# A two-layer decoder step on one core: the set-up block folded into the first layer, first cache pages loaded during the last prompt head, values applied by head groups, and each value page handed back by its own products

## What is computed

```python
def pool_layer(x, buf, ...):             # layer A: D_MODEL 1024, D_A 2048
    u, z = split(rmsnorm(x) @ w_in)      # 1024 x 4096
    mix = multiscale_pool(concat(buf, u))          # trailing windows 2/4/8/16
    mix = (mix by 4 groups @ w_map) * scale
    return x + (mix * silu(z)) @ w_out, last 15 rows of concat(buf, u)
k, v = split(rmsnorm(x) @ w_kv)          # shared K/V, rows are outputs too
def diff_layer(x, k, v):                 # layer B, 8 heads of 2 x 64 (k) and 128 (v)
    q, z = split(rmsnorm(x) @ w_in_b)
    p1, p2 = softmax(q1 k1 - alibi), softmax(q2 k2 - alibi)
    o = (p1 - lam * p2) @ v
    return x + (rmsnorm(o) * silu(z)) @ w_out_b
y = rmsnorm(x) * gain                    # samples attend to cache_k/v[page_table]
```

## Time and profile before

| | us |
|---|---|
| three timed runs | 3292.47, 3285.68, 3284.3 |
| their median | 3285.68 |
| the profiled execution, its own time | 3285.73 |
| its span, first to last instruction | 3283.9 |
| PE busy | 3091.5 (94%) |
| DVE, ACT, POOL busy | 1668.1, 1278.5, 96.6 |
| mean granted TensorE clock, share of full speed | 0.971 |

### The profile page before, as it was taken

One profiled execution on the slowest core, in us unless ns is written; L12 is line 12 of the kernel. 1 busy time (PEld: TensorE's weight loads), 2 busy tenths in 40 slices (PEclk: granted clock), 3 DMA queues, 4 the chain that ended last, 5 costly groups with the idle time before them and its releaser, 6 DMA issues. The chain is left out here.

```text
span 3283.9 us, 45647 instructions
## 1 busy us (share of the span) xinstructions
PE 3091.5 (94%) x17320; PEld 2571.3 (78%) x17320; DVE 1668.1 (51%) x2804; ACT 1278.5 (39%) x2291; POOL 96.6 (3%) x109
## 2 busy tenths in 40 slices
PE   5999999999989999899999999989999999786698
PEld 4888888889977888688888888779999998443586
DVE  4564655565453111244343433278888888332554
ACT  3333333333222000243333432267777777232322
POOL 0000000000000000000000000010000000000121
PEclk8999999999999999999999999989999999897799
DMA  4333333334315232255555554564444440797353
GB/s 142 132 118 128 122 114 132 106 118 155 124 47 190 92 102 86 93 188 184 189 177 180 171 181 160 163 137 91 104 104 110 110 104 15 291 335 283 105 177 108
DMA packets 266884, 465.59 MB, mean 142 GB/s; under 512 B 21432, under 2 KB 121272, under 8 KB 260632
## 3 DMA queue, kind: packets, MB, share of 16 engines
q1 hardware_dynamic: 266703, 463.14, 44.0%
HBM read 360.86 MB, written 102.95 MB: 141 GB/s over the span
## 5 line engine op out<-in xcount | busy, mean ns | idle before, releaser
L1442 ACT ACTIVATE attn_scores<-attn_scores,attn_lowest 128x1024 f32<-128x1024 f32 (+15 forms) x256 | 306.8, 1202 | 12.1 <-DVE attn_lowest L1495 12.1
L1495 DVE CUSTOM_DVE_ANT_0 attn_scores<-attn_s,region_early 128x1024 f32<-128x1024 f32 (+7 forms) x256 | 216.8, 856 | 107.8 <-POOL region_early L1348 38.1
L295 PE MATMUL pool_acc<-pool_odd_x_hi,pool_wh 128*128 128x272 f32 (+1 forms) x768 | 249.1, 324 | 0.0
L296 PE MATMUL pool_acc<-pool_odd_x_lo,pool_wh 128*128 128x272 f32 (+1 forms) x768 | 248.5, 324 | 0.0
L297 PE MATMUL pool_acc<-pool_odd_x_hi,pool_wl 128*128 128x272 f32 (+1 forms) x768 | 248.3, 323 | 0.0
L295 PE MATMUL outa_acc<-outa_w_hi,outa_g_hi 128*128 128x512 f32 (+1 forms) x544 | 213.8, 393 | 20.9 <-DVE outa_w_lo L775 17.8
L296 PE MATMUL outa_acc<-outa_w_lo,outa_g_hi 128*128 128x512 f32 (+1 forms) x544 | 213.1, 392 | 0.0
L297 PE MATMUL outa_acc<-outa_w_hi,outa_g_lo 128*128 128x512 f32 (+1 forms) x544 | 213.0, 391 | 0.0
L295 PE MATMUL pool_acc<-even_x,pool_wh 128*128 128x512 f32 x512 | 203.6, 398 | 1.4 <-DVE even_x L273 1.4
L297 PE MATMUL pool_acc<-even_x,pool_wl 128*128 128x512 f32 x512 | 201.7, 394 | 0.0
L296 PE MATMUL pool_acc<-even_x,pool_wh 128*128 128x512 f32 x512 | 200.2, 391 | 0.0
(11 more groups left out here) (253 smaller groups left out, 7185.7 us busy)
## 6 DMA issues: line engine op xcount, KB each, us to landing
pool_wu<-in_w_in_a SPq DMA_DIRECT2D x16, 2048.0 KB, 8.5
pool_wz<-in_w_in_a SPq DMA_DIRECT2D x16, 2048.0 KB, 8.5
region_early<-in_w_kv SPq DMA_DIRECT2D x16, 2048.0 KB, 9.3
region_early<-in_w_in_b SPq DMA_DIRECT2D x16, 2048.0 KB, 8.8
smp_k_page<-in_cache_k SPq DMA_DIRECT2D x64, 512.0 KB, 5.3
smp_v_page<-in_cache_v SPq DMA_DIRECT2D x64, 512.0 KB, 5.7
pool_wm<-in_w_map_a SPq DMA_DIRECT2D x16, 1024.0 KB, 5.5
region_early<-gatedT SPq DMA_DIRECT2D x16, 1024.0 KB, 5.5
```

The costliest lines, as they stand in the source:

```text
L295: pe.matmul(out, ah, bh, start=first, stop=False)
L296: pe.matmul(out, ah, bl, start=False, stop=False)
L1442: act.activation(part, part, ACT.Exp, scale=-1.0, bias=low[s][:, x:x + 1], accum_out=sums[s][:, i:i + 1]).then_inc(expd, 1)
L1495: dve.tensor_tensor_reduce(sc[s][:, c, a0:a0 + n], s_ps[idx % 2][:, 0:n], bias[h % 2][:, b0:b0 + n], -SCALE, low[s][:, x - 2:x - 1] if x > ...
```

## The change

Six edits, made together:

1. `setup` is gone. Its loads, transposes and small sums move into `PoolLayer.run`: POOL makes the identity first, the norm no longer waits for `ext`, the state is transposed after units 0 to 3 of the first quarter, lambda and the window table are made later. SP issues block 3 of x, `wz` and `wm` before the state, the lambdas and the columns. The weight splits come later in the order of the first norms.
2. The tails are transposed after units 5 and 6 of the last quarter, and stored before its last two gated stores.
3. `OutLayer`: weights are split per k and the first gated block in two pieces; the sample rows are multiplied in plain fp32 with four column groups side by side, 8 products behind each weight chunk while blocks 0 and 1 run, and the 96 products at the end are gone. A weight buffer is now reloaded only when these products have read it too.
4. `attention` places v and bias differently; during its last head SP loads the sample rows, the 8 key pages and 4 value pages of sequence 0.
5. `sample_attention`, with `v_order` = page 0, the new rows, pages 1 to 7: values by groups of two heads, one accumulator for each group of 32 rows, so no fold, no second ACT copy; each page counts `v_free` and the load of the next sequence's page waits for that alone. The constants of DVE are made after the first pages. `turn_a` comes one page earlier.
6. The stores of sequence 6 are issued before `first_loads`. Tiles of the last layer lie elsewhere.

```diff
 # PoolLayer.run, SP
+            self.first_loads(sp)
             norm.load(sp, 3)
             self.load_w(sp, "z", 0)
             self.load_w(sp, "m", 0)
+            sp.dma_start(state, D["state_pool"][0]...).then_inc(state_in, 16)
...
 # PoolLayer.run, PE
+            def turn_state(g):
+                if g == 0:
+                    pe.wait_ge(state_in, 16)
+                    pe.wait_ge(norm.lo, 2 * first_block[1])
...
+                if q == 0 and i < NG:
+                    turn_state(i)
+                if q == QN - 1 and i in (5, 6):
+                    turn_tails(2 * (i - 5))
+                    turn_tails(2 * (i - 5) + 1)
 # OutLayer.run, SP
             for i in range(2, KC // LK):
-                sp.wait_ge(w_lo, i - 1)
+                sp.wait_ge(w_lo, (i - 1) * LK)
+                sp.wait_ge(sample_mm, i - 1)
                 self.load_w(sp, i)
 # OutLayer.run, DVE: ahead of the first add
+            dve.wait_ge(sample_mm, KC // LK)
+            dve.wait_ge(xr_in, 16 * CG)
+            dve.tensor_tensor(xr[:, :], sample_acc[:, :], xr[:, :], ALU.add).then_inc(sample_added, 1)
 # OutLayer.run, PE
+            def sample_product(i):
+                pe.wait_ge(w_sem[i % 2], 16 * (i // 2) + 16)
+                for r in range(LK):
+                    k = i * LK + r
+                    for j in range(CG):
+                        last = pe.matmul(sample_acc[j * rest:(j + 1) * rest, :], gs[:, k, :], wst[i % 2][:, r, j * QN:(j + 1) * QN],
+                                         start=k == 0, stop=k == KC - 1)
+                last.then_inc(sample_mm, 1)
...
-            product(pairs, 0, rest)
 # attention, SP, last head
+                elif h == H - 1:
+                    if n == 0:
+                        sp.wait_ge(nxt.tab_in, 16)
+                        sp.wait_ge(scored, h * NP * NX)
+                    if n < nxt.NPG // 2:
+                        nxt.load(sp, "k", 0, 2 * n)
+                        nxt.load(sp, "k", 0, 2 * n + 1)
+                    elif n == nxt.NPG // 2:
+...
+                        for g in range(nxt.V_FIRST):
+                            nxt.load(sp, "v", 0, g)
 # sample_attention, SP
-                if not first:
-                    sp.wait_ge(applied, 2 * b)
-                for g in range(NPG):
-                    load_page(sp, table, D["cache_v"], b, g, vp, v_in)
+                for i, g in enumerate(v_order):
+                    sp.wait_ge(v_free, (b - 1) * (NPG + 1) + 1 + i)
...
             load_v(NB - 1)
+            store(NB - 2)
             nxt.first_loads(sp)
-            store(NB - 2)
             store(NB - 1)
 # sample_attention, PE
+            def apply(b):
...
+                for i, g in enumerate(v_order):
+                    if g < NPG:
+                        pe.wait_ge(v_in[g], 16 * b + 16)
+                    n = P if g < NPG else TS
+                    for j in range(CG):
+                        cols = slice(j * PAIR * P, (j + 1) * PAIR * P)
+                        v = vp[:, g, cols] if g < NPG else vnew[:, cols]
+                        x = pe.matmul(o_ps[j * QUADRANT:(j + 1) * QUADRANT, :], aT[0:n, g * HR:(g + 1) * HR], v,
+                                      start=i == 0, stop=i == NPG)
+                    x.then_inc(v_free, 1)
```

More of the change, by code:

```diff
@@ L86 @@
 LAMBDA_INIT = 0.8 - 0.6 * math.exp(-0.3 * LAYER_B)
[L89 to L143, removed]
-                for j in range(4):
-                    t = pe.transpose(pt[q % 2][:, j, 0:rows], state[:, (4 * q + j) * P:(4 * q + j + 1) * P],
-                                     K["ident"][0:rows, 0:rows])
-                t.then_inc(turned, 1)
-        @block.vector
-        def _(dve):
-            for q in range(NFB // 4):
-                dve.wait_ge(turned, q + 1)
-                dve.tensor_copy(K["stateT"][:, 4 * q:4 * q + 4, :], pt[q % 2][:, :, 0:rows]).then_inc(taken, 1)
-            dve.wait_ge(lam_in, 64)
-            for j in range(2):
-                dve.tensor_tensor_reduce(junk[:, :], vec[2 * j][:, :], vec[2 * j + 1][:, :], 1.0, 0.0, ALU.mult, ALU.add,
-                                         dot[:, j:j + 1]).then_inc(seq, 1)
-                dve.wait_ge(seq, j + 1)
-            dve.wait_ge(exped, 1)
-            dve.tensor_tensor(K["neglam"][:, :], ex[:, 1:2], ex[:, 0:1], ALU.subtract).then_inc(seq, 1)
-            dve.wait_ge(seq, 3)
-            dve.tensor_scalar(K["neglam"][:, :], K["neglam"][:, :], -LAMBDA_INIT, None, ALU.add)
-            dve.wait_ge(columns_in, 64)
-            dve.tensor_scalar(K["gain_v"][:, :], K["gain_v"][:, :], 1.0 - LAMBDA_INIT, None, ALU.mult)
[L166 to L169, removed]
@@ L273, in low @@
             dve.tensor_tensor(xl, bank, f32(xh), ALU.subtract).then_inc(self.lo, 1)
-def two_ahead(NB, ahead, behind, meanwhile, after=None):
-    for b in range(2):
-        ahead(b)
-    meanwhile()
-    for b in range(NB):
-        if b + 2 < NB:
-            ahead(b + 2)
-        behind(b)
-        if after:
-            after(b)
 FREE = 1
@@ L745, in split @@
                     act.wait_ge(mm, 2 * i + s - 1)
-                act.activation(gh[s][:, :, 0:n], gst[s][:, :, 0:n], ACT.Copy).then_inc(g_hi, 1)
-            split(0, 0, P)
-            for i in range(KC // LK):
-                if i == 1:
-                    split(0, 1, P)
+                act.activation(gh[s][:, first:, :], gst[s][:, first:, :], ACT.Copy).then_inc(g_hi, 1)
+            act.wait_ge(g_sem[0], 16)
+            act.activation(gh[0][:, 0:LK, :], gst[0][:, 0:LK, :], ACT.Copy).then_inc(g_begun, 1)
@@ L1912, in first_loads, with last_layer @@
         sp.dma_start(self.gf[:, :], self.D["norm_f_g"].partition_broadcast(P)).then_inc(self.gf_in, 16)
-def last_layer(nc, D, K, full, rest, H, early):
+def last_layer(nc, D, K, full, rest, H, early, below):
     w = D["w_out_b"][0]
```

510 lines of the change are left out of this document (312 added, 198 removed).

## The result

| | before | after |
|---|---|---|
| median of the timed runs, us | 3287.72 (4 runs, 3284.3 to 3292.47) | 3212.92 (4 runs, 3212.06 to 3214.32) |
| profiled execution: own time, span | 3285.73, 3283.9 | 3212.88, 3211.1 |
| mean granted TensorE clock | 0.971 | 0.983 |

The account below looks back on a forecast made before the run. PE, busy 94% of the span, was taken as the bound outside a few stretches, with SP nearly always working in the sample loop. Terms summed to -82.3 us against the profiled 3285.73, giving 3203.4; range 3186 to 3224.

Parts of the forecast that it names:

- Moved transposes, +4: Pool layer: 16 state and 16 tail transposes now run among PE's products; 32 were to take 3.7 us, so +4.
- Sample products +7.9: Out layer: 128 records of 256 columns at 0.061 us each, 7.8 us of PE, entered as +7.9.
- weight waits +4: Out layer: about every second chunk waits 1.1 to 1.6 us for its reloaded weight buffer; +4, bounds 0 and +12.
- add +0.8: Out layer: DVE's first add stands behind the last sample product; gap before second pair grows from 3.06 to 3.9 us.
- End of the out layer -22.2 and +1.1: Out layer: 96 narrow fp32r products gone, -22.2 us; last store of 128 rows instead of 32 and six more semaphores, +1.1.
- Sample stage -43.3: Sample stage: SP sets the loop at 24.9 us per sequence; last layer starts at 3007.0 instead of 3050.29; bounds -60 and -35.
- rivals 2: Sample loop gains nothing, 26 us per sequence, and SP holds the end 5 us longer; 3214 us, chance 0.14.
- 4 (3213): Front is bound by data: block 3 of x lands at 22, state late by 4 us; 3213 us, chance 0.10.
- Transfers as the bound (3185): Sample loop: page transfers, not SP, set the period at 21.2 us instead of 24.9; 3185 us, chance 0.08.
- Weight waits for every chunk, 17: Out layer: every chunk waits for weights, 7 x 2.5 = 17 us instead of 4; 3216 us, chance 0.12.
- Serialised hand-off, slower: Sample loop: page-wise releases make loads and products wait in turn, 44 us per sequence instead of 24.9; 3317 us, chance 0.03.
- Narrow products without overlap: Out layer and sample values: four column groups do not overlap, 0.24 us each; 3265 us, chance 0.03.

## Why the prediction was right, and where it was off

The mechanism of the large terms (front, seam, end of the out layer, SP's list in the sample stage) was right. The 9.5 us by which the sum was too good lie to two thirds in the second term, which was mis-sized, and to one third in the sample stage. In the first pair of the out layer two errors partly cancelled, +2.2 for the sample products and -1.7 for the weight waits; that was luck.

1. **Front, -23.6; measured -24.3.** Block 3 issued at 11.13 and the state hidden, as worked out.
2. **Moved transposes, +4; measured +10.0 for the phase. This is the step that failed most.** It counted PE's records alone. The wait for DVE's tail copies (1.56) and the steps into and out of each group make the tails 3.9 and the state 1.2 to 1.6. And 4.9 belong to no transpose: the new lambda tile moved the weight parts by 1312 bytes. The 1920 products of the two even parts took 0.0032 us more each in the mean (those on the mixed tiles included), the 960 of the odd part 0.0026 less, the 1920 narrower ones of the last part 0.0007 more: 6.2 - 2.5 + 1.3, about 5. The prediction had no term for the layout of the pool layer at all.
3. **Seam -7.3, out start -3.7; measured -7.0 and -3.8.**
4. **Sample products +7.9, weight waits +4, add +0.8; measured 10.1, 2.3 and 0.9, 0.8 more is not placed.** The step between records was better than the narrow row gave (0.046 against 0.061), but entering and leaving the narrow form costs about 0.5 us per chunk, 4 in all. The prediction had put 1.6 on it and had left it out of the sum: the 0.1 us that it read is one lengthened step, while in the trace before the change the 64 narrow records of the earlier trace rows (0.027 apart) already cost 0.4 us beyond themselves, way in and way out together. The Trainium skill, "TensorEngine Tiling (Array Packing)", section Key Properties, says that a change of mode drains the engine; the 0.5 us here fit that. Not every second chunk waited for 1.1 to 1.6 us, but five of the seven for 0.3 to 0.6 and one for 0.07.
5. **End of the out layer -22.2 and +1.1; measured -21.0.**
6. **Sample stage -43.3; measured -40.1.** SP's list as the bound held (25.14 against 24.9), and the key pages of sequence 3 came 49.2 us into the stage, 48.8 forecast; the value pages of sequence 7 came 1.4 late, and the end took 36.0 instead of 34.2 us. Two reasons given for the gain did not hold. Four pages instead of 24 ahead of the loop were to bring SP's lead; the preload brings 4.3, and the rest comes from PE going through the first sequences in 19.0 us. The release by page brings nothing; what is left is the form of the product.
7. **Rivals.** The time, 3212.9, is that of the rivals 2 (3214) and 4 (3213), but their mechanisms are not what happened: SP's period was 25.14 and not 26 and the end 1.8 us longer and not 5, and the first product came at 22.95 with no wait for the state. Transfers as the bound (3185): not in this kernel. Without the comparisons SP's list still came first (20.7), without the table PE (19.0), with the transfers falling behind. Weight waits for every chunk, 17: no. Serialised hand-off, slower: no. Narrow products without overlap: no, 0.046 a record.

## What to carry to other kernels

When a loop's pages are addressed by a register, count every instruction of the issuing queue beside its transfers: here 80 per sequence were 22 us of the kernel. A long row of products has a pace that here depended on where its two operands lie; compare the mean step of the products before and after whenever a tile is added or dropped, and try both operands at the same 64-byte phase. Read the granted clock behind each wait before a wait is given a price: shortening one by 2.3 us gave 4.0 here.

## What the runs showed of the hardware that was not expected

- The step of a 512-column fp32r product on x was 0.233 us where the weights and the moving data began at different 64-byte phases, and 0.2275 to 0.230 where they began at the same one, in four kernels (391 against 397 ns of one product's records); a shift of 32 bytes of one tile was enough.
- The DMA engines moved 418 GB/s over whole sequences, where 397 was the most seen before; asked for 442, they fell behind, and the time to landing went from 8.5 to 14.9 us.
- Five register instructions of a page load took SP 0.28 us, 0.057 each, in a load that needs 1.19 to 1.26 us of SP in all, of which the issue is 0.33.
- Behind a wait of 3.96 us the granted clock was 0.70 over the next 5.6 us (first products 0.43 apart at the level of 1.2 GHz, then 0.23 at 2.4 GHz); behind one of 1.70 it was 1.00.
